# Windowed attention of eight heads: one head at a time against pairs of heads from the two key groups

## The reference

```python
def swa_gqa_sinks(q, k, v, sinks):
    qb = q.reshape(B, N, W, G, R, dh)          # N=2 blocks of W=128, G=2 groups, R=4 heads each, dh=64
    kk, vv = ...                               # previous block and own block of keys, values
    s = jnp.einsum('bnigrd,bnjgd->bgrnij', qb, kk) * (dh ** -0.5)
    s = s - slopes * dist                      # slope of head h: 2 ** -(h + 1)
    s = jnp.where(blk_valid, s, -jnp.inf)
    m = jnp.maximum(jnp.max(s, axis=-1), sink)
    p = jnp.exp(s - m)
    p = p / (jnp.sum(p, axis=-1) + jnp.exp(sink - m))
    out = jnp.einsum('bgrnij,bnjgd->bnigrd', p, vv)
    return out.reshape(B, T, Hq * dh)
y_s = swa @ w_swa_out
```

## Time and profile before

| | |
|---|---|
| median of 3 runs | 919.49 us (916.34 to 919.61) |
| profiled execution, its own time | 918.26 us |
| profiled execution, span from the first to the last instruction | 916.4 us |
| TensorE busy | 901.9 us (98%) |
| TensorE weight loads | 820.7 us (90%) |
| VectorE busy | 656.2 us (72%) |
| ScalarE busy | 492.8 us (54%) |
| granted TensorE clock, mean | 0.996 |

### The profile page before, as it was taken

The page is one execution under the profiler, slowest core; times in us unless marked ns, Lnnn a source line. Parts: engine busy times, 40 slices in busy tenths (PEclk is TensorE's granted clock), DMA queues, the critical chain, the costliest instruction groups (busy, mean ns, idle before and its releaser), DMA issues.

```text
span 916.4 us, 17024 instructions
## 1 busy us (share of the span) xinstructions
PE 901.9 (98%) x6286; PEld 820.7 (90%) x6286; DVE 656.2 (72%) x1101; ACT 492.8 (54%) x769; POOL 0.2 (0%) x4
## 2 busy tenths in 40 slices
PE   8999999999999999999999999999999999999997
PEld 4478888888899999999999998999999889999996
DVE  4977688888886876676677988876576766555555
ACT  4632566666664755555556545445464664444443
POOL 0000000000000000000000000000000000000000
PEclk9999999999999999999999999999999999999999
DMA  9858644443425265655655543345446356555551
GB/s 338 314 188 315 258 139 138 139 137 137 137 92 185 83 215 172 199 177 170 200 178 166 182 143 126 129 162 176 159 150 215 129 186 205 185 187 189 187 185 51
DMA packets 45582, 160.86 MB, mean 176 GB/s; under 512 B 5216, under 2 KB 6624, under 8 KB 45408
## 3 DMA queue, kind: packets, MB, share of 16 engines
q1 hardware_dynamic: 43488, 156.27, 50.3%
q10 hardware_dynamic: 2048, 3.97, 1.2%
HBM read 159.16 MB, written 1.05 MB: 175 GB/s over the span
## 4 chain that ended last, share of the span: by engine, by line
PE 86%; DVE 4%; DMA 4%; ACT 3%; issue 2%; SPq 0%; DVEq 0%; ACTq 0%
PE bank L439 21%; PE bank L441 20%; PE bank L440 20%; PE bank L505 4%; PE bank L507 4%; PE bank L506 4%; DMA raw<-in_stream 2%; DMA arena<-in_ada 2%; DVE arena L1592 1%; PE bank L1265 1%; ACT w_hi L426 1%; PE bank L1307 1%; PE bank L1287 1%; PE bank L1303 1%; PE bank L1267 1%
## 5 line engine op out<-in xcount | busy, mean ns | idle before, releaser
L433 DVE TENSOR_TENSOR w_lo<-raw,w_hi 128x1024 fp32r<-128x1024 f32 x252 | 304.3, 1222 | 133.8 <-ACT w_hi L426 133.3
L439 PE MATMUL bank<-h_hi,w_hi 128*128 128x256 f32 (+1 forms) x1232 | 369.5, 300 | 2.8 <-DVE w_lo L433 1.9
L441 PE MATMUL bank<-h_hi,w_lo 128*128 128x256 f32 (+1 forms) x1232 | 363.1, 295 | 0.0
L440 PE MATMUL bank<-h_lo,w_hi 128*128 128x256 f32 (+1 forms) x1232 | 361.6, 293 | 0.0
L426 ACT ACTIVATE w_hi<-raw 128x1024 fp32r<-128x1024 f32 x252 | 261.1, 1051 | 133.6 <-PE bank L441 86.9
L439 PEld LDWEIGHTS bank<-h_hi,w_hi 128*128 128x128 f32 x1232 | 232.3, 189 | 13.1 <-issue 2.9
L440 PEld LDWEIGHTS bank<-h_lo,w_hi 128*128 128x128 f32 x1232 | 234.1, 190 | 6.4
L441 PEld LDWEIGHTS bank<-h_hi,w_lo 128*128 128x128 f32 x1232 | 231.6, 188 | 5.8
L439 PE MATMUL bank<-y_hi,w_hi 128*128 128x256 f32 x304 | 86.6, 285 | 0.0
L441 PE MATMUL bank<-y_hi,w_lo 128*128 128x256 f32 x304 | 86.0, 283 | 0.0
L440 PE MATMUL bank<-y_lo,w_hi 128*128 128x256 f32 x304 | 85.4, 281 | 0.0
(11 more groups left out here) (259 smaller groups left out, 1118.4 us busy)
## 6 DMA issues: line engine op xcount, KB each, us to landing
raw<-in_stream SPq DMA_DIRECT2D x252, 512.0 KB, 3.4
arena<-in_ada SPq DMA_DIRECT2D x32, 512.0 KB, 5.2
xres<-in_ada SPq DMA_DIRECT2D x8, 512.0 KB, 3.3
tok<-in_tok SPq DMA_DIRECT2D x3, 512.0 KB, 8.5
con<-in_con ACTq DMA_DIRECT2D x1, 1472.0 KB, 9.8
xres<-in_tok ACTq DMA_DIRECT2D x1, 1024.0 KB, 8.5
out<-arena SPq DMA_DIRECT2D x4, 256.0 KB, 2.1
tok<-in_tok SPq DMA_DIRECT2D x2, 256.0 KB, 10.1
```

The source lines that it names most:

```text
L433: dve.tensor_tensor(w_lo[c.slot][:, :], raw[c.slot][:, :], w_hi[c.slot][:, :].bitcast(F32), ALU.subtract).then_inc(S("split_lo"), 1)
L439: pe.matmul(dst, hi_w, a_hi, start=start, stop=False, skip_group_check=True)
L440: pe.matmul(dst, hi_w, a_lo, start=False, stop=False, skip_group_check=True)
L441: return pe.matmul(dst, lo_w, a_hi, start=False, stop=stop, skip_group_check=True)
```

## The change

The heads are worked in another order: step number e now does head `head_of(e)` = 0, 4, 1, 5, 2, 6, 3, 7. So two neighbouring steps are heads of the two key groups with the same columns of s_q. TensorE does the scores of both at the tile of the even step: the short matmul of group 0 and of group 1 into banks 5 and 6, then the long ones of both. Value products are done at the tile of the odd step for both: group 0 into partitions 0 to 63 of bank 4, group 1 into 64 to 127, short after long. Scores therefore come behind tiles 6, 10, 14 and 18, value products behind tiles 12, 16, 20 and 24. VectorE copies both results of a pair out of bank 4 in one instruction of 128 partitions. Transposes, exponentials and norms stay one head at a time, where they were. Waits are recounted to pairs: the scores of a pair wait for the biases of the whole pair before, the copy of probabilities for the value product of the pair before. On the host the rows of w_swa_out are put into the same order of heads.

```diff
--- before.py
+++ after.py
@@ -154,6 +154,11 @@
 
     e, odd = divmod(t - SWA_FIRST - after, 2)
     return e if odd == 0 and 0 <= e < S_HEADS else None
+
+
+def head_of(e):
+
+    return 4 * (e % 2) + e // 2
 
 
 def ret_at(t, after):
@@ -1022,7 +1027,7 @@
                     act.activation(gate_dst(t), gate_dst(t), ACT.Sigmoid).then_inc(S("gate"), 1)
 
             def softmax_exp(e):
-                p = e % 2
+                p, head = e % 2, head_of(e)
                 act.wait_ge(S("s_neg"), e + 1)
                 if e >= 2:
                     act.wait_ge(S("p_turned"), e - 1)
@@ -1030,12 +1035,12 @@
                                accum_out=s_sum[p][:, 0:1]).then_inc(S("s_exp"), 1)
                 act.activation(s_p[p][:, P:3 * P], s_b[p][:, P:3 * P], ACT.Exp, scale=S_DH ** -0.5,
                                bias=s_neg[p][:, 1:2], accum_out=s_sum[p][:, 1:2]).then_inc(S("s_exp"), 1)
-                act.activation(s_sink[p], s_neg[p], ACT.Exp, bias=sink[:, e:e + 1]).then_inc(S("s_exp"), 1)
+                act.activation(s_sink[p], s_neg[p], ACT.Exp, bias=sink[:, head:head + 1]).then_inc(S("s_exp"), 1)
 
             def probs_copy(e):
                 act.wait_ge(S("p_turned"), e + 1)
                 if e >= 2:
-                    act.wait_ge(S("pv"), e - 1)
+                    act.wait_ge(S("pv"), e // 2)
                 act.activation(s_pT[e % 2], psum[7][:, 0:3 * P], ACT.Copy).then_inc(S("p_T"), 1)
 
             def ret_squares(r):
@@ -1074,7 +1079,7 @@
                 if e is not None:
                     probs_copy(e)
                 if swa_at(t, 6) == S_HEADS - 1:
-                    act.wait_ge(S("swa"), S_HEADS)
+                    act.wait_ge(S("swa"), S_HEADS // 2)
                     act.activation(h_hi[:, 8 * T:12 * T], swa, ACT.Copy).then_inc(S("swa_hi"), 1)
                     act.dma_start(post_mix, post_mix_in.partition_broadcast(P)).then_inc(S("post_mix_in"), 16)
                 if X_FIRST < t <= X_FIRST + 8 and (t - X_FIRST) % 2 == 1:
@@ -1426,16 +1431,19 @@
                 last.then_inc(S("v2_turned"), 1)
 
             def swa_scores(e):
-                g, x = e // 4, (e % 4) * T
-                rows = slice(S_DH * g, S_DH * g + S_DH)
+                x = e // 2 * T
                 if e == 0:
                     pe.wait_ge(S("in2_copied"), T_VS)
-                if e >= 2:
-                    pe.wait_ge(S("s_biased"), e - 1)
-                dst = psum[5 + e % 2]
-                pe.matmul(dst[:, 0:P], s_q[rows, x:x + P], s_k[rows, 0:P], start=True, stop=True, skip_group_check=True)
-                pe.matmul(dst[:, P:3 * P], s_q[rows, x + P:x + T], s_k[rows, 0:T], start=True, stop=True,
-                          skip_group_check=True).then_inc(S("s_scores"), 1)
+                else:
+                    pe.wait_ge(S("s_biased"), e)
+                for g in range(2):
+                    rows = slice(S_DH * g, S_DH * g + S_DH)
+                    pe.matmul(psum[5 + g][:, 0:P], s_q[rows, x:x + P], s_k[rows, 0:P], start=True, stop=True,
+                              skip_group_check=True)
+                for g in range(2):
+                    rows = slice(S_DH * g, S_DH * g + S_DH)
+                    pe.matmul(psum[5 + g][:, P:3 * P], s_q[rows, x + P:x + T], s_k[rows, 0:T], start=True, stop=True,
+                              skip_group_check=True).then_inc(S("s_scores"), 1)
 
             def turn_probs(e):
                 pe.wait_ge(S("p_norm"), 2 * e + 2)
@@ -1446,16 +1454,21 @@
                 last.then_inc(S("p_turned"), 1)
 
             def swa_values(e):
-                g, q = e // 4, S_DH * (e % 2)
+                pair = e // 2
                 pe.wait_ge(S("p_T"), e + 1)
-                if e == 0:
+                if pair == 0:
                     pe.wait_ge(S("v2"), 1)
-                if e >= 2:
-                    pe.wait_ge(S("swa"), e - 1)
-                pe.matmul(psum[4][q:q + S_DH, 0:T], s_v[:, S_DH * g:S_DH * g + S_DH], s_pT[e % 2][:, 0:T],
-                          start=True, stop=False, skip_group_check=True)
-                pe.matmul(psum[4][q:q + S_DH, P:T], s_v[:, P + S_DH * g:P + S_DH * g + S_DH], s_pT[e % 2][:, T:3 * P],
-                          start=False, stop=True, skip_group_check=True).then_inc(S("pv"), 1)
+                else:
+                    pe.wait_ge(S("swa"), pair)
+                for g in range(2):
+                    q = S_DH * g
+                    pe.matmul(psum[4][q:q + S_DH, 0:T], s_v[:, q:q + S_DH], s_pT[g][:, 0:T], start=True, stop=False,
+                              skip_group_check=True)
+                for g in range(2):
+                    q = S_DH * g
+                    last = pe.matmul(psum[4][q:q + S_DH, P:T], s_v[:, P + q:P + q + S_DH], s_pT[g][:, T:3 * P], start=False,
+                                     stop=True, skip_group_check=True)
+                last.then_inc(S("pv"), 1)
 
             def turn_x(n):
                 pe.wait_ge(S("residual"), 3 * KT)
@@ -1481,7 +1494,7 @@
             def ret_values(r):
                 pe.wait_ge(S("r_sc"), r + 1)
                 if r == 0:
-                    pe.wait_ge(S("swa"), S_HEADS)
+                    pe.wait_ge(S("swa"), S_HEADS // 2)
                     pe.wait_ge(S("v_step"), 3)
                 else:
                     pe.wait_ge(S("r_gated"), r)
@@ -1518,9 +1531,12 @@
                     turn_values(t - 1)
                 if X_FIRST <= t < X_FIRST + 8 and (t - X_FIRST) % 2 == 0:
                     turn_x((t - X_FIRST) // 2)
-                for after, step in ((0, swa_scores), (3, turn_probs), (4, swa_values)):
-                    if swa_at(t, after) is not None:
-                        step(swa_at(t, after))
+                if swa_at(t, 0) is not None and swa_at(t, 0) % 2 == 0:
+                    swa_scores(swa_at(t, 0))
+                if swa_at(t, 3) is not None:
+                    turn_probs(swa_at(t, 3))
+                if swa_at(t, 4) is not None and swa_at(t, 4) % 2 == 1:
+                    swa_values(swa_at(t, 4))
                 for after, step in ((0, ret_scores), (2, ret_values), (4, ret_sum)):
                     if ret_at(t, after) is not None:
                         step(ret_at(t, after))
@@ -2006,7 +2022,8 @@
             def softmax_max(e):
 
                 p = e % 2
-                slope = 2.0 ** (-8.0 / S_HEADS * (e + 1))
+                head = head_of(e)
+                slope = 2.0 ** (-8.0 / S_HEADS * (head + 1))
                 dve.wait_ge(S("s_scores"), e + 1)
                 if e >= 2:
                     dve.wait_ge(S("s_exp"), 3 * (e - 1))
@@ -2016,7 +2033,7 @@
                 dve.reduce_max(s_max[p][:, 0:1], s_b[p][:, 0:P], AX)
                 dve.reduce_max(s_max[p][:, 1:2], s_b[p][:, P:3 * P], AX).then_inc(S("s_max"), 1)
                 dve.wait_ge(S("s_max"), e + 1)
-                dve.tensor_scalar(s_neg[p], s_max[p], -(S_DH ** -0.5), sink_neg[:, e:e + 1], ALU.mult,
+                dve.tensor_scalar(s_neg[p], s_max[p], -(S_DH ** -0.5), sink_neg[:, head:head + 1], ALU.mult,
                                   ALU.min).then_inc(S("s_neg"), 1)
 
             def softmax_norm(e):
@@ -2030,9 +2047,9 @@
                     dve.tensor_scalar(s_p[p][:, x], s_p[p][:, x], s_den[p][:, b:b + 1], None, ALU.mult).then_inc(S("p_norm"), 1)
 
             def swa_copy(e):
-                q = S_DH * (e % 2)
-                dve.wait_ge(S("pv"), e + 1)
-                dve.tensor_copy(swa[q:q + S_DH, (e // 2) * T:(e // 2 + 1) * T], psum[4][q:q + S_DH, 0:T]).then_inc(S("swa"), 1)
+                pair = e // 2
+                dve.wait_ge(S("pv"), pair + 1)
+                dve.tensor_copy(swa[:, pair * T:(pair + 1) * T], psum[4][:, 0:T]).then_inc(S("swa"), 1)
 
             def ret_decay(r):
                 dve.wait_ge(S("r_scores"), r + 1)
@@ -2084,9 +2101,11 @@
                     centre_values()
                 if T_GR <= t - 2 < T_GS:
                     silu(t - 2)
-                for after, step in ((1, softmax_max), (2, softmax_norm), (5, swa_copy)):
+                for after, step in ((1, softmax_max), (2, softmax_norm)):
                     if swa_at(t, after) is not None:
                         step(swa_at(t, after))
+                if swa_at(t, 5) is not None and swa_at(t, 5) % 2 == 1:
+                    swa_copy(swa_at(t, 5))
                 if swa_at(t, 7) == S_HEADS - 1:
                     dve.wait_ge(S("swa_hi"), 1)
                     dve.tensor_tensor(h_lo[:, 8 * T:12 * T], swa, h_hi[:, 8 * T:12 * T].bitcast(F32),
@@ -2244,6 +2263,7 @@
     r_q, r_k, r_v, r_g, s_q, s_k, s_v, g_r, g_s = (w2[:, i:j] for i, j in zip(edges[:-1], edges[1:]))
     s_q = s_q.reshape(D, 2, 4, S_DH).transpose(0, 2, 1, 3).reshape(D, 512)
     in2 = _columns(np.concatenate([s_q, s_k, s_v, r_q, r_k, r_v, r_g, g_s, g_r], axis=1))
+    swa_out = a["w_swa_out_2"][0].reshape(2, 4, S_DH, D).transpose(1, 0, 2, 3).reshape(512, D)
```

(2 more changed lines are left out.)

## The result

| | |
|---|---|
| median of 7 runs | 909.37 us (909.0 to 913.64) |
| kernel before, 7 runs beside them | 918.4 us (916.34 to 919.61) |
| ratio | 0.9913, 95% interval 0.9896 to 0.9931 |
| the change again (experiment 9) | 910.69 us (6 runs) against 918.63, ratio 0.9912, interval 0.989 to 0.9935 |
| profiled execution, and its span | 909.77 us, 908.0 us |

A forecast was written before the change was run, and what follows sets the result against it. TensorE's own queue was taken as the bound; attention blocks falling from 14.1 to 7.2 us save 6.9, so 918.26 - 6.9 = 911.4, or 912.6 against the 919.49 median. Range: 910 to 917.5 us.

The forecast's parts named there:

- TensorE alone sets the pace: Attention, tiles 6 to 24: TensorE busy 71.77 of 71.77 us, so time taken from its queue comes off the end.
- The price of blocks: Half-array blocks between weight matmuls, without tile 24: 14.1 us before, 7.2 after (scores 1.05, values 1.00 each); saved 6.9.
- Overlap of column halves: Value products: two heads on the two 64-column halves run side by side, a block staying at 1.00 us.
- Overlap of row halves: Scores: two heads on the two row halves run side by side, 1.05 us a block; 1.69 if not.
- rival 3: Score blocks: row halves do not overlap, columns do; 4 x 0.64 = 2.6 us less saved, 915.2 us; chance 0.08.
- rival 2: Score blocks: row halves load weights one after another, 4 x 0.24 = 1.0 us less saved, 913.6 us; chance 0.12.
- Rival 5: Paired blocks: each of 24 half switches costs 0.20 us, nothing overlaps; 922.5 us; chance 0.04 with anything else slower.
- Rival 1: Paired blocks: passes start in program order, second half trails 0.21 us a block; 1.7 us lost, 914.3 us; chance 0.11.
- VectorE's cover: VectorE's waiting for TensorE over four tiles, 567.58 to 584.27 us: 1.97 us before, 0.7 left after; nothing charged.
- The size: Whole kernel: 6.9 us saved, 911.4 us against the profiled execution, 912.6 against the median of three runs.

The follow-up runs named there:

- experiment 9: The change once more, unaltered, in more rounds: 910.69 us (6 runs) against 918.63 for the kernel before, ratio 0.9912.
- experiment 2: Against the kernel before, only value products paired, scores one head at a time: ratio 0.9962 to the kernel before.
- experiment 5: The change, but both heads' value products go through the lower 64 columns of the array: one run, 916.92 us.
- experiment 1: Against the kernel before, only scores paired, value products one head at a time: ratio 0.9955 to the kernel before.
- experiment 3: The change, but both heads of a pair take their scores from the lower 64 rows: ratio 0.9947 to the kernel before.
- experiment 6: The change with the four score matmuls of each pair issued nine times over: ratio 1.0153 to the kernel before.
- experiment 7: The change with each pair's scores issued nine times over, both heads from the lower 64 rows: ratio 1.0395 to the kernel before.
- experiment 4: The change with both matmuls of the lower half first in the program, then both of the upper, for scores and values: ratio 0.9927 to the kernel before.
- experiment 8: The change with the first two pairs' value products moved two tiles back, behind tiles 14 and 18: ratio 0.9939 to the kernel before.

## Why the prediction was right

- **TensorE alone sets the pace.** Right: 64.07 of 64.07 us busy, no wait of TensorE in the stretch, and everything behind it moved with it (321.57 us to the end before, 321.62 after).
- **The price of blocks.** 14.1 us before and 7.2 after were forecast; after, the score blocks cost 1.04 to 1.05, the value blocks 0.98 to 1.00, tile 24's 1.65 against 1.64.
- **Overlap of column halves,** read from L1276: shown by experiments 2 and 5. **Overlap of row halves,** which no row showed and which was argued from the nearest one: shown by experiments 1, 3, 6 and 7. Here the prediction was a bet that came in; the four 0.64 us of rival 3 hung on it. The weight loads of row halves overlap as well: two loads start together, so rival 2's 0.24 a block is not there.
- **No cost of switching halves.** Rival 5 asked for 0.20 at each of 24 switches; a score block with three switches costs 1.04, as one head alone did before.
- **The rivals' order of starts.** Rival 1 was to cost 1.7 us, and nothing of it came. In experiment 4 the fifth and sixth passes of the program (L1441, upper half) start before the third (L1443, lower half). The rule of the Trainium skill, "TensorE: Matmul & The Clock Gate", Part 3, The mechanism, that matmuls start and end in program order, does not hold across halves in this trace.
- **VectorE's cover.** 0.7 us of waiting were to be left in four tiles with all their work; 0.7 is what the list of waits has from 557.5 to 572.6 us. That they agree owes something to the choice of tiles. In the four tiles from tile 14's block to tile 18's the kernel before waits only 0.8 us for TensorE (554.2 to 570.7 us) and not 1.97, and in the kernel after (549.9 to 565.0 us) VectorE waits for TensorE nowhere, only once for ScalarE:

```profile
DVE w_lo L438 <- ACT w_hi L431: 0.4, 1, 0.4
```

  There the cover is used up, and TensorE does not notice, as the prediction said of such a case. So the cover was thinner than the sum of one stretch of tiles let it seem, and experiment 8 shows what lies behind it. The four copies saved are 1.7 us of VectorE's work, as forecast; its busy time in the page fell by 2.8, and the rest is not explained.
- **The size.** 6.9 us is what the profile shows between equal points. The two comparisons give 8.0 and 8.1, whose intervals (from 6.3 and from 6.0) hold 6.9. What the sum did not foresee is the distance to the medians. 909.37 us is 3.2 us below the 912.6 that was forecast against the first median, and 0.6 below the lower end of the range, 910. 1.1 of the 3.2 is the kernel before, whose median was 919.49 in three runs and 918.4 in seven; 2.1 is left. The 1.4 us that the range allowed for runs lying lower was too small. Only 6 of the change's 13 runs and 8 of the 40 of the kernel before with a clock on record have a mean granted clock of 0.999 or 1.000. These took 909.5 us on average (908.44 to 910.28) and 916.2 (915.48 to 917.36), 6.7 us apart. So I take what goes beyond 6.9 for the draw of the first 120 us, where the change happened to have more of the quick runs. That is argued from few runs, not shown.

## What to carry to other kernels

Matmuls that use only 64 rows or 64 columns of the array cost a second head nothing here when the other half's matmuls stand next to them in the queue, in both of the orders in which they were written. To find what it brings, count half-array blocks, not matmuls: here a block cost 0.64 us of streaming for each head and product and 0.35 to 0.40 of entering and leaving, and of the 6.9 us saved 5.1 are streaming and 1.8 the fewer entries. Move steps to pair them only where the engine behind them keeps its lead: two tiles' delay of a 1 us step (experiment 8) cost 2.6 us.

## What the runs showed of the hardware

Two things were not expected. First, overlap on row halves is as complete as it can be told: 0.655 us a round for two heads, where the streaming of one is 0.64 to 0.65. Second, nearly all the scatter between the traces of this kernel comes from its first 120 us. The table by stretches for 94 to 104 us, of the kernel before, of the change, and of the kernel of experiment 8:

```profile
94.00:104.00 10.00, 9.26 (x67) 9.18 (x67) 3.97 (x7) 3.84 (x6) 0.00 (x0) 0.83 0.75 296
```

```profile
94.00:104.00 10.00, 9.71 (x82) 9.38 (x80) 5.19 (x7) 5.29 (x7) 0.00 (x0) 1.00 0.81 319
```

```profile
94.00:104.00 10.00, 7.63 (x43) 7.10 (x42) 4.94 (x7) 3.40 (x3) 0.00 (x0) 0.68 0.89 330
```

In the same program text the granted clock was 0.83, 1.00 and 0.68 on average over these 10 us: for part of them it stood at 0.50, the 1.2 GHz level, in the first and the third, as from 98 to 100 us of the kernel before:

```profile
98.00:100.00 2.00, 2.00 (x11) 2.00 (x11) 0.00 (x0) 0.00 (x0) 0.00 (x0) 0.50 1.05 416
```

The eleven traces fall into three groups by this clock. With 1.00 from 94 to 104 us (the change, experiments 1, 3 and 6) the first L1281 starts at 117.4 to 118.3 us, with 0.83 (before, 2, 4 and 9) at 119.9 to 121.0, with 0.66 to 0.68 (5, 7 and 8) at 122.2 to 123.5. So the clock in these 10 us goes with the 6 us by which the executions differ before the attention starts; tile 6's block began at 523.92, 522.27 and 527.58 us in the three shown. Why the clock falls in some executions stays open. TensorE had waited there for weights (in the kernel of experiment 8 for 2.6 us of w_lo, in the kernel before for 1.2, in the change for 0.8), with the DMA engines busy for over nine tenths of the time ahead of it, in the change too. But the kernels of experiments 3 and 6 waited 1.2 us for w_lo as well, and their clock stayed at 1.00. The profile of before had lost 1.65 us by tile 6's block against that of after, which is why the two spans differ by 8.4 and not by 6.9.
